# Where the last attention's shift and scale vectors are computed: VectorE in the second layer's MLP, or TensorE in the pooled layer's MLP

## The chip, the cores and the metric

The program runs on one core of a Trainium2 chip, in one launch. The metric is the device time of that core in microseconds (us), from the start of the program to its end; lower is better.

## The reference, cut to what matters

Two transformer blocks follow each other on 256 tokens of width 1024, all in float32. The first block has two layers (sparse attention, differential attention), the second has two as well: a pooling mixer, whose layer treats two streams of tokens (latent and context), and a grouped-query attention that reads both. Each layer has an MLP of its own. What is modulated is computed from a conditioning vector:

```python
mod = jax.nn.silu(c) @ ada_w[i] + ada_b[i]                                   # first block, one stream
sh1, sc1, g1, sh2, sc2, g2 = jnp.split(s_lat @ ada_w[i] + ada_b[i], 6, axis=-1)      # second block, latent
csh1, csc1, cg1, csh2, csc2, cg2 = jnp.split(s_ctx @ ada_w[i] + ada_b[i], 6, axis=-1)  # second block, context
a_l = modulate(rms_norm_2(h_lat, norm_g[i, 0]), sh1, sc1)
a_c = modulate(rms_norm_2(h_ctx, norm_g[i, 0]), csh1, csc1)
y_c, y_l = attn_mix(a_c, a_l, attn_w_qkv[j], attn_w_o[j], attn_q_g[j], attn_k_g[j], ctx_out)
```

So every layer needs six vectors of 1024 numbers, each the product of a vector of 1024 with a 1024x1024 matrix: 24 such products (numbered 0 to 23 below, six for each layer). For the last layer, vectors 18 and 19 (shift and scale ahead of the attention) are wanted for both streams, `c_2` and `c_ctx_2`; 20 to 23 for the latent stream alone.

## The kernel before, in words

The five engines run programs written by hand, with semaphores between them; nothing is reordered by a scheduler. The heavy work is a stream of weight **units** of 1 MB (128 partitions x 2048 floats). A unit goes through four stages: SyncE's queue loads it into one of four raw slots (`wraw`, `RAW_SLOTS`), ScalarE rounds it to `whi` (line 638, two halves), VectorE writes the rest `wlo = wraw - whi` (line 1161, two halves), and TensorE multiplies with three matmuls per product (high by high, high by low, low by high: lines 1980 to 1982). There are three slots for `whi` and `wlo`, so ScalarE may split unit u + 3 once TensorE has done unit u.

The MLPs are the segments `up0`, `down0` (first layer), `up1`, `down1` (second layer, 22 and 11 units), `up20`, `down20` (pooled layer, latent stream, 16 and 16), `up21`, `down21` (pooled layer, context stream) and `up3`, `down3` (last layer). Between `down1` and `up20` stand the two pooling products. `stream` is the loop of ScalarE and of VectorE over the units of a segment, `up_segment` and `down_segment` that of TensorE.

The 24 vector products are done in the gaps, in two ways. A product needs 4 MB of weights, in four pieces of 1 MB that take raw slots of the same ring as the units.
- By TensorE (`vector_units`, line 1927): a piece is 8 matmuls in plain fp32 with 32 columns, `cpad` (the conditioning vector, column 0 latent and column 1 context) against the raw weights; the four quarters of the output stand in four column groups of the array. TensorE waits for the piece to land, and the slot is free when the matmuls are done. Both streams come out of the same matmuls.
- By VectorE (`vector_rows`, lines 1104 and 1106, the vectors in `BY_VECTOR`): a piece is two instructions over 128x1024, which multiply a row block by the partition's number of `cpad` and add it to an accumulator in `work`. After four pieces `rows_sum` on TensorE (line 1908) adds up the partitions by 4 matmuls with the constant `first`.
Either way `vector_out` on VectorE (line 1086) then adds the bias to the result in PSUM bank 7 and writes `modrow`, and `columns` turns shift and scale to columns.

Where this happens is a table by hand: `HOSTED` (units of a segment after which a piece runs on TensorE), `ROWED` (VectorE's pieces), `SUMMED` (after which unit `rows_sum` comes) and `ADDED` (when `vector_out` comes). The function `hosting` sets by the same tables where in SyncE's queue (in order) the piece's transfer stands: for a piece at unit i, behind the transfer of unit i + 3. Before the change, vectors 18 and 19 are the eight pieces `HOSTED` in `up20`, at units 3, 4, 5, 6, 8, 9, 10 and 11. `up1` and `down1` hold no pieces.

## Time and profile before

| what | value |
|---|---|
| median of 3 runs | 1567.08 us (1566.0 to 1568.85) |
| the profiled execution | 1567.17 us, of which the span from first to last instruction is 1565.4 us |
| TensorE (matmul) busy | 1468.5 us (94%) |
| VectorE busy | 966.7 us (62%) |
| ScalarE busy | 759.3 us (49%) |
| mean granted TensorE clock | 0.979 |
| `up1`, from its zeroing matmul to that of `down1` | 568.2 to 699.0 us |
| `up20`, likewise | 807.0 to 923.0 us |
| `up21`, likewise | 1015.1 to 1112.2 us |

In the profile, busy matmul time overlaps: the duration of one is from its start to its modelled end, and several are in flight. What a unit costs is therefore read from the distance between events of neighbouring units. ScalarE's split of unit u + 3 is released by TensorE's last matmul of unit u, so the starts of line 638 in the timeline mark the ends of units on TensorE.

### The profile page before, as it was taken

To read this page: it belongs to the slowest core of one execution; us is meant where nothing else is said; L and a number is where in the kernel's file an instruction comes from. 1 tells how busy PE (TensorE), PEld (TensorE's weight loads), DVE (VectorE), ACT (ScalarE), POOL (GpSimd) and SP (SyncE) were. 2 spreads that over 40 slices of the span, in tenths; PEclk is the share of its full clock that TensorE was granted. 3 is DMA by queue.
4 is the path that set the end of the run, shared out by engine and by line. 5 is a ranking of instruction groups with operands and counts; after the bars stand their busy time and mean duration, and the time that the engine had idled before them with its cause. 6 is when DMAs were issued, how large, how long until landed. Compare 5 with 4: busy or idle time off the path is not lost.

```text
span 1565.4 us, 23725 instructions
## 1 busy us (share of the span) xinstructions
PE 1468.5 (94%) x9784; PEld 1250.5 (80%) x9784; DVE 966.7 (62%) x1537; ACT 759.3 (49%) x1197; POOL 22.1 (1%) x44
## 2 busy tenths in 40 slices
PE   4998899999999799999998999999999979899997
PEld 2775689998786589998877888799887756699886
DVE  3687565657787764456774447755577774554455
ACT  3525563334553554346464356455654535465543
POOL 1000000000000000000000000000000000000000
PEclk9999999999999799999999999999999989999999
DMA  9884787767757676554487955767466630255551
GB/s 348 277 280 162 245 268 248 264 237 288 287 183 274 259 253 224 176 179 156 137 295 273 320 189 213 267 210 247 166 229 228 215 108 1 81 162 188 170 200 48
DMA packets 174123, 334.76 MB, mean 214 GB/s; under 512 B 9656, under 2 KB 115648, under 8 KB 173888
## 3 DMA queue, kind: packets, MB, share of 16 engines
q1 hardware_dynamic: 172512, 331.52, 61.6%
q8 instruction: 78, 1.28, 0.3%
q0 software_dynamic: 1504, 1.72, 0.3%
q14 instruction: 29, 0.24, 0.0%
HBM read 332.17 MB, written 1.05 MB: 213 GB/s over the span
## 4 chain that ended last, share of the span: by engine, by line
PE 82%; DVE 10%; ACT 3%; DMA 3%; issue 2%; SPq 0%; DVEq 0%; ACTq 0%
PE ps L1980 24%; PE ps L1981 23%; PE ps L1982 23%; DVE wlo L1161 2%; PE ps L1927 2%; DMA wraw<-in_ada_w_dram 2%; PE ps L2178 1%; PE ps L2123 1%; DMA work<-in_ada_w_dram 1%; DVE res L1281 1%; DVE work L1279 1%; PE ps L2120 1%; ACT whi L638 1%; PE ps L2246 1%; PE ps L2210 1%
## 5 line engine op out<-in xcount | busy, mean ns | idle before, releaser
L1161 DVE TENSOR_TENSOR wlo<-wraw,whi 128x1024 fp32r<-128x1024 f32 (+1 forms) x424 | 497.4, 1216 | 321.3 <-ACT whi L638 320.8
L638 ACT ACTIVATE whi<-wraw 128x1024 fp32r<-128x1024 f32 (+1 forms) x424 | 421.7, 1045 | 383.2 <-PE ps L1982 347.7
L1980 PE MATMUL ps<-hT_hi,whi 128*128 128x256 f32 x1472 | 420.1, 285 | 0.5 <-DVE hT_lo L1353 0.5
L1981 PE MATMUL ps<-hT_lo,whi 128*128 128x256 f32 x1472 | 417.0, 283 | 0.0
L1982 PE MATMUL ps<-hT_hi,wlo 128*128 128x256 f32 x1472 | 416.9, 283 | 0.0
L1980 PEld LDWEIGHTS ps<-hT_hi,whi 128*128 128x128 f32 x1472 | 282.9, 192 | 9.1 <-issue 7.1
L1981 PEld LDWEIGHTS ps<-hT_lo,whi 128*128 128x128 f32 x1472 | 283.0, 192 | 0.0
L1982 PEld LDWEIGHTS ps<-hT_hi,wlo 128*128 128x128 f32 x1472 | 282.9, 192 | 0.0
L1980 PE MATMUL ps<-whi,act_hi 128*128 128x512 f32 x560 | 219.7, 392 | 0.0
L1982 PE MATMUL ps<-whi,act_lo 128*128 128x512 f32 x560 | 218.0, 389 | 0.0
L1981 PE MATMUL ps<-wlo,act_hi 128*128 128x512 f32 x560 | 217.9, 389 | 0.0
L1980 PE MATMUL ps<-whi,hT_hi 128*128 128x512 f32 (+2 forms) x416 | 162.7, 391 | 15.2 <-DVE hT_lo L1353 10.3
L1981 PE MATMUL ps<-wlo,hT_hi 128*128 128x512 f32 (+2 forms) x416 | 159.7, 384 | 0.0
L1982 PE MATMUL ps<-whi,hT_lo 128*128 128x512 f32 (+2 forms) x416 | 159.2, 383 | 0.0
L1980 PEld LDWEIGHTS ps<-whi,act_hi 128*128 128x128 f32 x560 | 105.1, 188 | 25.0 <-issue 3.7
L658 ACT ACTIVATE act_hi<-work 128x512 fp32r<-128x512 f32 x70 | 44.0, 629 | 164.9 <-PE ps L1982 164.9
L1168 DVE TENSOR_TENSOR act_lo<-work,act_hi 128x512 fp32r<-128x512 f32 x70 | 48.4, 692 | 121.7 <-ACT act_hi L658 121.4
L1982 PEld LDWEIGHTS ps<-whi,act_lo 128*128 128x128 f32 x560 | 105.1, 188 | 22.0
L1981 PEld LDWEIGHTS ps<-wlo,act_hi 128*128 128x128 f32 x560 | 105.1, 188 | 21.5
L1980 PEld LDWEIGHTS ps<-whi,hT_hi 128*128 128x128 f32 x416 | 79.9, 192 | 35.9 <-DVE hT_lo L1353 11.0
L1982 PEld LDWEIGHTS ps<-whi,hT_lo 128*128 128x128 f32 x416 | 79.8, 192 | 15.2
L1981 PEld LDWEIGHTS ps<-wlo,hT_hi 128*128 128x128 f32 x416 | 80.0, 192 | 14.3
(259 smaller groups left out, 1289.1 us busy)
## 6 DMA issues: line engine op xcount, KB each, us to landing
wraw<-in_mlp_w_dram SPq DMA_DIRECT2D x96, 1024.0 KB, 5.4
wraw<-in_ada_w_dram SPq DMA_DIRECT2D x78, 1024.0 KB, 5.7
wraw<-in_ffn_w_gate_dram SPq DMA_DIRECT2D x22, 1024.0 KB, 6.2
wraw<-in_ffn_w_up_dram SPq DMA_DIRECT2D x22, 1024.0 KB, 5.8
wraw<-in_ffn_w_down_dram SPq DMA_DIRECT2D x22, 1024.0 KB, 4.9
work<-in_ada_w_dram SPq DMA_DIRECT2D x18, 1024.0 KB, 9.9
wraw<-in_diff_w_in_dram SPq DMA_DIRECT2D x12, 1024.0 KB, 5.8
wraw<-in_attn_w_qkv_dram SPq DMA_DIRECT2D x12, 1024.0 KB, 5.2
```

The costliest lines, as they stand in the source:

```text
L638: nc.scalar.activation(whi[:, u % SPLIT_SLOTS, part], raw_view("w", u)[:, part], ACT.Copy).then_inc(hi_ready, 1)
L658: nc.scalar.activation(act_hi[:, d % 2, :], hid[:, 512 * i:512 * i + 512], ACT.Copy).then_inc(act_hi_ready, 1)
L1161: nc.vector.tensor_tensor(wlo[:, u % SPLIT_SLOTS, part], raw_view("w", u)[:, part], whi[:, u % SPLIT_SLOTS, part].bitcast(F32), ALU.subtra ...
L1168: nc.vector.tensor_tensor(act_lo[:, d % 2, :], hid[:, 512 * i:512 * i + 512], act_hi[:, d % 2, :].bitcast(F32), ALU.subtract).then_inc(act ...
L1279: nc.vector.tensor_tensor(tmp[:, t, cols], ps[:, D_BANKS[q], :], gate_b[:, cols], ALU.mult).then_inc(dve_emptied, 1)
L1281: nc.vector.tensor_tensor(res[:, strm, t, cols], res[:, strm, t, cols], tmp[:, t, cols], ALU.add).then_inc(sem("res_ready"), 1)
L1927: ins = mm(ps[32 * c_:32 * c_ + 32, ADA_BANK, 0:256], cpad[:, 0 if g < 12 else 1, kt, :], raw_view("a", r)[:, kk * D + 256 * c_:kk * D + 2 ...
L1980: mm(dst, s_hi, m_hi, start=start, stop=False, skip_group_check=skip)
L1981: mm(dst, s_hi, m_lo, start=False, stop=False, skip_group_check=skip)
L1982: return mm(dst, s_lo, m_hi, start=False, stop=stop, skip_group_check=skip)
L2120: ins = mm(ps[:, t_bank(n, b), (k % 2) * S:(k % 2 + 1) * S], xn[:, t, k * P:(k + 1) * P], mats[:, b, t, :], start=(t == 0), stop=(t == TT ...
L2123: ins = nc.tensor.transpose(ps[:, t_bank(n, b), (k % 2) * S + t * P:(k % 2) * S + (t + 1) * P], xn[:, t, k * P:(k + 1) * P], ident)
```

## The change

Vectors 18 and 19 join `BY_VECTOR`, with a row sum of their own for each stream (`BOTH`): a piece is now four VectorE instructions, two for each stream, and the sum is 8 matmuls in place of 4. `HOSTED` is gone. The pieces stand in `up1` (units 3, 6, 9, 12, 15, 18) and `down1` (units 5, 7), with the sums after unit 14 of `up1` and unit 9 of `down1`. As 18 and 19 now come ahead of 16 and 17, `IN_TURN` holds the new order of all vectors, for the waits on `mod_rows` and for the bias loads on GpSimd's queue. The constant `first` gets a 33rd column, so that a slice of it puts the sum in row 0 or row 1 of each group of 32. The two sums of a group of 32 columns follow each other directly (`for c_ ... for strm ...`). In `down20` and `down21` the sum moves from after unit 13 to after unit 14, its `vector_out` from 14 to 15.

```diff
-    put("first", np.tile((np.arange(32) == 0).astype(np.float32), (P, 1)))
+    put("first", np.tile((np.arange(33) == 1).astype(np.float32), (P, 1)))
...
-        BY_VECTOR = (7, 8, 9, 20, 21, 22, 23)
+        BY_VECTOR = (7, 8, 9, 18, 19, 20, 21, 22, 23)
+        BOTH = (18, 19)
+        IN_TURN = list(range(16)) + [18, 19, 16, 17, 20, 21, 22, 23]
...
-        HOSTED = {"up20": (3, 4, 5, 6, 8, 9, 10, 11)}
-        ROWED = {"up0": (3, 5, 7, 9, 11, 13, 15, 16), "down0": (0, 2, 4, 6), "up20": (3, 5, 7, 9), "down20": (6, 8, 10, 12),
+        ROWED = {"up0": (3, 5, 7, 9, 11, 13, 15, 16), "down0": (0, 2, 4, 6), "up1": (3, 6, 9, 12, 15, 18), "down1": (5, 7), "up20": (3, 5, 7, 9), "down20": (6, 8, 10, 12),
                  "up21": (2, 4, 6, 8), "down21": (6, 8, 10, 12)}
-        SUMMED = {"up0": (11, 18), "down0": (8,), "up20": (13,), "down20": (13,), "up21": (10,), "down21": (13,)}
-        ADDED = {"up0": (12, 19), "down0": (9,), "up20": (7, 12, 14), "down20": (14,), "up21": (11,), "down21": (14,)}
+        SUMMED = {"up0": (11, 18), "down0": (8,), "up1": (14,), "down1": (9,), "up20": (13,), "down20": (14,), "up21": (10,), "down21": (14,)}
+        ADDED = {"up0": (12, 19), "down0": (9,), "up1": (15,), "down1": (10,), "up20": (14,), "down20": (15,), "up21": (11,), "down21": (15,)}
...
+        def row_sums(g, strm):
+            return wk(5632 + 1024 * strm if g in BOTH else 11264 - 1024 * (BY_VECTOR.index(g) % 2), 1024)
...
-                if j == 0 and r >= 8:
+                if j == 0 and g == 19:
+                    dve.wait_ge(sem("rows_summed"), r // 4)
+                elif j == 0 and r >= 8:
                     dve.wait_ge(sem("rows_summed"), r // 4 - 1)
...
+                    for strm in range(2 if g in BOTH else 1):
+                        acc = row_sums(g, strm)
+                        by = cpad[:, 0 if g < 12 else 1, kt, strm:strm + 1]
+                        if kt == 0:
+                            ins = nc.vector.tensor_scalar(acc, w, by, None, ALU.mult)
+                        else:
+                            ins = nc.vector.scalar_tensor_tensor(out=acc, in0=w, scalar=by, in1=acc, op0=ALU.mult, op1=ALU.add)
...
+                strms = 2 if g in BOTH else 1
                 for c_ in range(4):
-                    ins = mm(ps[32 * c_:32 * c_ + 32, ADA_BANK, 0:256], const("first"), acc[:, 256 * c_:256 * (c_ + 1)], start=True, stop=True)
+                    for strm in range(strms):
+                        ins = mm(ps[32 * c_:32 * c_ + 32, ADA_BANK, 0:256], const("first")[:, 1 - strm:33 - strm], row_sums(g, strm)[:, 256 * c_:256 * (c_ + 1)],
+                                 start=(strm == 0), stop=(strm == strms - 1))
...
-                    if i in HOSTED.get(name, ()):
-                        vector_units()
```

On TensorE, between units 3 and 4 of `up20`, stood the first of the eight pieces. Before:

```order
L1982 MATMUL ps<-hT_hi,wlo 128x256
L1927 MATMUL ps<-wraw,cpad 32x256 [waits raw_full1,mod_ready,mod_rows]
L1927 MATMUL ps<-wraw,cpad 32x256 x7
L1980 MATMUL ps<-hT_hi,whi 128x256 [waits hact_done,lo_ready]
L1981 MATMUL ps<-hT_lo,whi 128x256
```

After, at the same place:

```order
L1990 MATMUL ps<-hT_lo,whi 128x256
L1991 MATMUL ps<-hT_hi,wlo 128x256
L1989 MATMUL ps<-hT_hi,whi 128x256 [waits hact_done,lo_ready]
L1990 MATMUL ps<-hT_lo,whi 128x256
L1991 MATMUL ps<-hT_hi,wlo 128x256
```

The eight matmuls and their wait for a landing are gone, here and at seven more places of `up20`.

On VectorE, in `up1` at unit 12, the split of the weights (`wlo`) is followed by the columns of an earlier vector (`modT`, `modA`). Before:

```order
L1161 TENSOR_TENSOR wlo<-wraw,whi 128x1024 [waits hi_ready] x2
L1143 COPY modT<-ps 128x2x4 [waits ada_turn]
L1143 COPY modT<-ps 128x2x4 x3
L1147 SCALAR_TENSOR_TENSOR modA<-modT,paramT 128x8 [waits dve_chain]
L1147 SCALAR_TENSOR_TENSOR modA<-modT,paramT 128x8
L1161 TENSOR_TENSOR wlo<-wraw,whi 128x1024 [waits hi_ready,mod_ready]
```

After:

```order
L1168 TENSOR_TENSOR wlo<-wraw,whi 128x1024 [waits hi_ready] x2
L1113 SCALAR_TENSOR_TENSOR work<-wraw,cpad,work 128x1024 [waits raw_full2]
L1113 SCALAR_TENSOR_TENSOR work<-wraw,cpad,work 128x1024
L1113 SCALAR_TENSOR_TENSOR work<-wraw,cpad,work 128x1024 [waits dve_chain]
L1113 SCALAR_TENSOR_TENSOR work<-wraw,cpad,work 128x1024
L1150 COPY modT<-ps 128x2x4 [waits ada_turn,rows_used]
L1150 COPY modT<-ps 128x2x4 x3
L1154 SCALAR_TENSOR_TENSOR modA<-modT,paramT 128x8 [waits dve_chain]
```

Four instructions and a wait for a landed piece stand ahead of the columns and of the next split.

On SyncE's queue, in `up1`, the transfers of the weights (`ffn_w_gate`, `ffn_w_up`) were alone. Before:

```order
L562 DMA wraw<-in_ffn_w_gate_dram 128x8x256 [waits lo_ready]
L562 DMA wraw<-in_ffn_w_up_dram 128x8x256 [waits lo_ready]
L562 DMA wraw<-in_ffn_w_gate_dram 128x8x256 [waits lo_ready]
L562 DMA wraw<-in_ffn_w_up_dram 128x8x256 [waits lo_ready]
L562 DMA wraw<-in_ffn_w_gate_dram 128x8x256 [waits lo_ready]
```

After:

```order
L579 DMA wraw<-in_ada_w_dram 128x2x1024 [waits lo_ready]
L566 DMA wraw<-in_ffn_w_up_dram 128x8x256 [waits lo_ready]
L566 DMA wraw<-in_ffn_w_gate_dram 128x8x256 [waits lo_ready]
L566 DMA wraw<-in_ffn_w_up_dram 128x8x256 [waits lo_ready]
L579 DMA wraw<-in_ada_w_dram 128x2x1024 [waits rows_used]
L566 DMA wraw<-in_ffn_w_gate_dram 128x8x256 [waits lo_ready]
```

Every fourth transfer is now a piece of the vectors, and from the second on it waits for VectorE to be done with the piece before it.

## Rows read from the trace of the kernel before

**Rows 1.** The page: busy time by engine, and the chain that ended last.
```profile
PE 1468.5 (94%) x9784; PEld 1250.5 (80%) x9784; DVE 966.7 (62%) x1537; ACT 759.3 (49%) x1197; POOL 22.1 (1%) x44
...
PE 82%; DVE 10%; ACT 3%; DMA 3%; issue 2%; SPq 0%; DVEq 0%; ACTq 0%
```
**Rows 2.** Windows: stretch, length, busy by engine, clock, DMA share, GB/s (`up1`, `up20`, `up21`).
```profile
568.20:699.00 130.80, 130.41 (x1074) 128.68 (x1073) 65.39 (x72) 59.10 (x71) 4.40 (x8) 1.00 0.65 214
...
807.00:923.00 116.00, 107.35 (x918) 98.46 (x918) 54.38 (x53) 56.72 (x77) 0.00 (x0) 0.99 0.79 272
...
1015.10:1112.20 97.10, 96.17 (x791) 93.92 (x791) 52.49 (x54) 51.09 (x67) 0.00 (x0) 1.00 0.66 217
```
**Rows 3.** Timeline of TensorE in `up20`: start, length, instruction, count of records, idle before.
```profile
833.21 1.07 PE L1927 MATMUL ps<-wraw,cpad 128*32 128x256 f32 x16
...
842.70 1.07 PE L1927 MATMUL ps<-wraw,cpad 128*32 128x256 f32 x16 [2.48 <-DMA wraw<-in_ada_w_dram]
...
858.91 1.07 PE L1927 MATMUL ps<-wraw,cpad 128*32 128x256 f32 x16 [2.25 <-DMA wraw<-in_ada_w_dram]
...
872.51 1.07 PE L1927 MATMUL ps<-wraw,cpad 128*32 128x256 f32 x16 [0.82 <-DVE modrow L1086]
...
888.64 1.93 PE L1927 MATMUL ps<-wraw,cpad 128*32 128x256 f32 x16 [2.17 <-DMA wraw<-in_ada_w_dram]
```
**Rows 4.** Windows again: the stretch around the last of these waits.
```profile
886.60:892.20 5.60, 3.56 (x24) 2.30 (x25) 2.36 (x2) 3.08 (x4) 0.00 (x0) 0.70 1.03 367
```
**Rows 5.** Timeline of ScalarE in `up20`: splits released by units 3, 4 and 12.
```profile
833.37 2.01 ACT L638 ACTIVATE whi<-wraw 128x1024 fp32r<-128x1024 f32 x2 [4.95 <-PE ps L1982]
840.31 2.00 ACT L638 ACTIVATE whi<-wraw 128x1024 fp32r<-128x1024 f32 x2 [2.81 <-PE ps L1982]
...
904.25 2.01 ACT L638 ACTIVATE whi<-wraw 128x1024 fp32r<-128x1024 f32 x2 [3.79 <-PE ps L1982]
```
**Rows 6.** Timeline of VectorE in `up1`, units 3 and 4.
```profile
596.19 2.36 DVE L1161 TENSOR_TENSOR wlo<-wraw,whi 128x1024 fp32r<-128x1024 f32 x2 [5.76 <-ACT whi L638]
598.47 0.69 DVE L1180 TENSOR_TENSOR work<-ps,hbuf 128x512 f32<-128x512 f32 x1
601.95 2.36 DVE L1161 TENSOR_TENSOR wlo<-wraw,whi 128x1024 fp32r<-128x1024 f32 x2 [2.80 <-ACT whi L638]
```
**Rows 7.** Timeline of ScalarE in `up0`, around a sum by 4 matmuls.
```profile
285.42 2.01 ACT L638 ACTIVATE whi<-wraw 128x1024 fp32r<-128x1024 f32 x2 [3.26 <-PE ps L1982]
291.94 2.01 ACT L638 ACTIVATE whi<-wraw 128x1024 fp32r<-128x1024 f32 x2 [4.51 <-PE ps L1982]
```
**Rows 8.** Timeline of TensorE: fp32 matmuls on two column groups, and on the whole array.
```profile
121.00 3.65 PE L2302 MATMUL ps<-wraw,work 128*32 128x256 f32 x32
...
777.42 7.07 PE L2120 MATMUL ps<-work 128*128 128x256 f32 x32
```
**Rows 9.** Instructions that read `cpad`: count, ns (least, median, most), first and last start.
```profile
L1106 DVE SCALAR_TENSOR_TENSOR work<-wraw,cpad,work x49: 1275/1284/1287, 244.1 to 1191.3; 128x1024 f32<-128x1024 f32 x49
```
**Rows 10.** The page, DMA issues: name, queue, count, KB each, us to landing.
```profile
wraw<-in_ada_w_dram SPq DMA_DIRECT2D x78, 1024.0 KB, 5.7
```
**Rows 11.** Timeline of VectorE, then of ScalarE, in `down1`, units 5 to 10.
```profile
743.03 0.69 DVE L1168 TENSOR_TENSOR act_lo<-work,act_hi 128x512 fp32r<-128x512 f32 x1 [3.20 <-ACT act_hi L658]
743.98 2.36 DVE L1161 TENSOR_TENSOR wlo<-wraw,whi 128x1024 fp32r<-128x1024 f32 x2 [0.26 <-ACT whi L638]
748.47 0.69 DVE L1168 TENSOR_TENSOR act_lo<-work,act_hi 128x512 fp32r<-128x512 f32 x1 [2.13 <-ACT act_hi L658]
...
769.12 0.68 DVE L1279 TENSOR_TENSOR work<-ps,gate_b 128x512 f32<-128x512 f32 x1
...
753.25 0.63 ACT L658 ACTIVATE act_hi<-work 128x512 fp32r<-128x512 f32 x1 [2.91 <-PE ps L1982]
```
**Rows 12.** Who waited for whom on TensorE, 990 to 1203 us: us, times, longest.
```profile
PE ps L1908 <- DVE work L1106: 2.4, 2, 1.2
```
**Rows 13.** Timeline of ScalarE at the end of `down21`: splits released by units 13 and 14.
```profile
1192.09 1.99 ACT L638 ACTIVATE whi<-wraw 128x1024 fp32r<-128x1024 f32 x2
1199.06 2.01 ACT L638 ACTIVATE whi<-wraw 128x1024 fp32r<-128x1024 f32 x2 [4.99 <-PE ps L1982]
```

More of the change, by code:

```diff
@@ L39 @@
 for _name, _n in (("ident", 128), ("causal", 256), ("cmp_neg", 32), ("cmp_ok", 32), ("ax_cos", 128), ("ax_sin", 128),
-                  ("inv_freq", 8), ("sel0", 128), ("sel1", 128), ("spread", 128), ("headmask", 512), ("first", 32)):
+                  ("inv_freq", 8), ("sel0", 128), ("sel1", 128), ("spread", 128), ("headmask", 512), ("first", 33)):
     CONST_COLS[_name] = (_at, _at + _n)
@@ L336, in hosting @@
             for i in range(by_name[name]["count"]):
-                if i in HOSTED.get(name, ()) or i in ROWED.get(name, ()):
+                if i in ROWED.get(name, ()):
                     units(by_name[name]["base"] + i + 4 - counted["w"])
-                if i in HOSTED.get(name, ()):
-                    extras(1)
                 if i in ROWED.get(name, ()):
@@ L366, in build @@
         extras(4)
+        hosting("up1")
+        hosting("down1")
         up_to("up20")
@@ L1044, in _ @@
                 bias(g)
-            for g in range(9, 21):
+            for g in IN_TURN[9:21]:
                 bias_after(g)
@@ L1077, in vector_out @@
                 for _ in range(n):
-                    g = vector_no[0]
+                    g = IN_TURN[vector_no[0]]
                     vector_no[0] += 1
@@ L1095, in vector_rows @@
                 raw_wait(dve, "v", r)
-                acc = wk(11264 - 1024 * (r // 4 % 2), 1024)
-                if j == 0 and r >= 8:
+                if j == 0 and g == 19:
+                    dve.wait_ge(sem("rows_summed"), r // 4)
+                elif j == 0 and r >= 8:
                     dve.wait_ge(sem("rows_summed"), r // 4 - 1)
@@ L1101, in vector_rows @@
                     w = raw_view("v", r)[:, kk * D:(kk + 1) * D]
-                    by = cpad[:, 0 if g < 12 else 1, kt, 0:1]
-                    if kt == 0:
-                        ins = nc.vector.tensor_scalar(acc, w, by, None, ALU.mult)
-                    else:
-                        ins = nc.vector.scalar_tensor_tensor(out=acc, in0=w, scalar=by, in1=acc, op0=ALU.mult, op1=ALU.add)
+                    for strm in range(2 if g in BOTH else 1):
[5 more added lines that the diff above has]
+                            ins = nc.vector.scalar_tensor_tensor(out=acc, in0=w, scalar=by, in1=acc, op0=ALU.mult, op1=ALU.add)
                     if kk == 0:
@@ L1903, in rows_sum @@
                 pe.wait_ge(sem("rows_used"), 4 * summed[0])
-                pe.wait_ge(mod_rows, g)
+                pe.wait_ge(mod_rows, IN_TURN.index(g))
                 bank7_wait()
-                acc = wk(11264 - 1024 * ((summed[0] - 1) % 2), 1024)
+                strms = 2 if g in BOTH else 1
                 for c_ in range(4):
-                    ins = mm(ps[32 * c_:32 * c_ + 32, ADA_BANK, 0:256], const("first"), acc[:, 256 * c_:256 * (c_ + 1)], start=True, stop=True)
+                    for strm in range(strms):
+                        ins = mm(ps[32 * c_:32 * c_ + 32, ADA_BANK, 0:256], const("first")[:, 1 - strm:33 - strm], row_sums(g, strm)[:, 256 * c_:256 * (c_ + 1)],
+                                 start=(strm == 0), stop=(strm == strms - 1))
                 ins.then_inc(sem("rows_summed"), 1)
@@ L1920, in vector_units @@
                         if g > 0:
-                            pe.wait_ge(mod_rows, g)
+                            pe.wait_ge(mod_rows, IN_TURN.index(g))
                         bank7_wait()
@@ L1965, in columns @@
                 assert EXTRA[extra_no[0] - 1][2] == 3 or EXTRA[extra_no[0] - 1] == ("cmp", 1, 1)
-                pe.wait_ge(mod_rows, last_vector[0] + 1)
+                pe.wait_ge(mod_rows, IN_TURN.index(last_vector[0]) + 1)
                 bank7_wait()
@@ L2056, in up_segment @@
                     hidden_unit(s_, i)
-                    if i in HOSTED.get(name, ()):
-                        vector_units()
                     if i in SUMMED.get(name, ()):
@@ L2170, in gate @@
                         emptied(n, t)
-                pe.wait_ge(mod_rows, 6 * l + 3 * f + 3)
+                pe.wait_ge(mod_rows, IN_TURN.index(6 * l + 3 * f + 2) + 1)
                 for h in range(2):
```

## The prediction, made before the changed kernel ran

> **What bounds the kernel now.** I first read the page: TensorE's matmuls are busy 94% of the span and make 82% of the chain that ended last, VectorE is busy 62% and ScalarE 49% [rows 1]. So a microsecond counts where it is TensorE's, work or wait; VectorE has room on the average, and the question is where. I then read windows over single MLPs [rows 2]. `up20` and `up21` are the same 16 units, but `up20` takes 116.0 us against 97.1, and TensorE is idle for 8.6 us of it. `up1` has nothing but its units: TensorE is busy for 130.4 of 130.8 us, VectorE for 65.4. The timeline of TensorE shows what is in the way in `up20` [rows 3]: the pieces of vectors 18 and 19, and ahead of four of them an idle time, 2.48, 2.25, 0.82 and 2.17 us. Three of the four end with the landing of the piece's own transfer. After the last, the granted clock is 0.70 over a stretch of 5.6 us [rows 4], and the same 16 records take 1.93 us in place of 1.07.
>
> **Part 1: the eight pieces leave `up20`.** The splits of ScalarE mark the ends of TensorE's units. From the end of unit 3 to that of unit 12 it is 904.25 - 833.37 = 70.88 us [rows 5], with nine units and all eight pieces between. A unit alone takes 5.76 us: in `up1`, VectorE's splits of neighbouring units start at 596.19 and 601.95 [rows 6]. Nine are 51.8 us, so the pieces cost 19.0. This divides into eight times 1.18 for the matmuls (the first piece: 840.31 - 833.37 - 5.76) or 9.4, the four idle times, 7.7, and 1.9 left over, mostly the low clock. All of it is between units on TensorE, with no cover: **-19.0 us**. Check: 116.0 - 19.0 = 97.0, and `up21`, which already has four one-stream pieces on VectorE, a sum and four transposes more, takes 97.1. The four pieces of vector 20 stay in `up20` and were there before.
>
> **Part 2: two sums come to TensorE's path.** A sum by 4 matmuls costs 0.76 us between units (291.94 - 285.42 - 5.76) [rows 7]. Eight matmuls in two rounds of four column groups cost 1.18, so a further round costs 0.42. That the round is one matmul long shows elsewhere: 16 matmuls (32 records, two each) on two column groups take 3.65 us, 0.46 for each pair, and 16 on the whole array 7.07, 0.44 each [rows 8]. The new sum has 8 matmuls, but in the order group 0, group 0, group 1, group 1 and so on. No row shows this order. Below: if group 1 may start while the second of group 0 waits, two rounds, 1.18. Above: one after the other, 0.34 + 8 x 0.44 = 3.9. I take the case in which a waiting matmul holds up those behind it: the second of a group then runs beside the first of the next, five rounds, 0.34 + 5 x 0.43 = 2.5. It is also about the middle. The sums stand between units, in `up1` after unit 14 and in `down1` after unit 9: **+5.0 us** (2.4 to 7.8). The Trainium skill ("TensorE: Matmul & The Clock Gate", Part 3, Packing small matmuls) states that matmuls are strictly first in, first out, in start and in end, and only weight loads are pulled ahead. By it a sum is 2.5 us and the total as here; if matmuls passed each other it would be 1.2 and the total 2.6 less. No row of this trace has the order that would tell.
>
> **Part 3: VectorE's pieces in `up1`, taken at nothing.** A piece is four instructions of 1.284 us [rows 9], 5.2 with the wait in its middle (the first of each vector is cheaper). Three units, the distance of two pieces, give VectorE 3 x 2.36 for splits, 1.5 x 0.69 for products and 5.2: 13.3 of 17.3 us. In detail at unit 3: it ends at 595.1 (half a split of ScalarE, 1.1, ahead of 596.19), VectorE is through with split and product at 599.15, the piece lasts to 604.3, and the split of unit 7, which stood at 601.95, ends at 606.7. TensorE wants it at 595.1 + 3 x 5.76 = 612.4. The cover is thus 5.7 us, and if it were gone, each microsecond over would be one of TensorE's. Behind the piece on VectorE stand that split and, at unit 12, the columns of vectors 12 and 13, which the sum after unit 14 waits for with 2 us to spare. On SyncE's queue a piece waits for its slot, from the second on for the piece before to be used, and the weights stand behind it. Unit 10's transfer takes the slot of unit 7, free at 606.7; with 5.7 us to land [rows 10] it is there at 612.4, wanted by ScalarE at the end of unit 7, 618.1. Again 5.7 us. GpSimd's bias loads in the new order wait for columns that are made before `up1` starts; ScalarE's program is the same. All at 0.
>
> **Part 4: VectorE's pieces in `down1`, taken at nothing.** Here a unit is 5.44 us (748.47 - 743.03) [rows 11] and the cover thinner. The split at 743.98 ends at 746.3, the piece at 751.5, and the rest of the activations of unit 8 (`act_lo`, at 748.47 before) at 752.3. TensorE wants it when unit 7 ends, at 753.2 (the start of ScalarE at 753.25): 0.9 us to spare. The second piece runs from 757.6 to 762.8, ahead of the end of unit 9 at 764.1, where the sum wants it, by 1.3. VectorE then comes to the residual some 1.0 us later than 769.12 (0.6 from late splits, 0.4 for `vector_out`). TensorE itself comes 2.5 later there because of the sum, counted above, so this adds nothing; if the sum were 1.2 it would just cover it.
>
> **Part 5: the sum moved in `down20` and `down21`.** TensorE waits there for VectorE's last piece, 1.2 us each time [rows 12]. One unit later the piece is long done. In `down20` the wait goes, 1.2. In `down21` units 13 and 14 stand 1199.06 - 1192.09 = 6.97 us apart [rows 13], 1.53 over 5.44; what follows is VectorE's split and residual, released by the end of unit 14, which now has no sum ahead of it: 1.5. `vector_out` stands in the same place of VectorE's program as before, since no split lies between: **-2.7 us** (0 to -3.1).
>
> **The sum.** -19.0 + 5.0 - 2.7 = -16.7 against the profiled execution's 1567.17 us, of which 1565.4 is span: 1550.5. The median is 0.1 below that execution, so **1550.4 us**.
>
> **The rivals.**
> A. The matmuls of the sums pass each other. For it: in rows 3 four groups run together, 16 records in 1.07. Against it: there each group's next matmul comes only after the other groups' first. Sums of 1.2: 1550.4 - 2.6 = 1547.8.
> B. VectorE holds up TensorE in `up1` or `down1`. For it: 0.9 us in `down1`, where the transfers, the splits and the pieces meet; against it: the 1284 ns vary by 12 at most over 49 instructions. Overruns of 2 to 6 us: 1552.4 to 1556.4.
> C. The change doesn't do what it says: the idle times of `up20` come from the ring of four slots, which vector 20's pieces still share, and not from the pieces on TensorE. Then 7.7 + 1.9 stay: 1560.0. Against it: `up21` has the same four pieces on the same ring, and its unit times add up to 97.1.
> D. Slower. In `up1` the weight transfers stand in SyncE's queue behind pieces that wait for VectorE. From the point at which a piece takes over 10.9 us on VectorE (5.2 and the cover of 5.7), TensorE pays the rest at each of eight places. Equal to before is reached 16.7 / 8 = 2.1 us later, at 13.0 us a piece, 2.5 times what rows 9 say; at 13.5 it would be 1571. Nothing in the rows speaks for it but the untried order of the queue.
>
> **The chances.** Forecast (1549.0 to 1552.4) 0.63; A 0.15; B 0.13; C 0.05; D 0.02; something unseen 0.02, half of it slower. The range that holds 8 in 10 takes in A and most of B: 1547.0 to 1555.0. A measurement of this kernel can tell about 0.2%, 3.1 us, from no change; faster by more than that 0.96, within it 0.01, slower 0.03.
>
> **What the changed profile would show.** Part 1: `up20` lasts 97 us, with no matmul on `cpad` in it and no idle time of TensorE over 0.5 us inside; the granted clock stays at 1.00. Part 2: the splits of ScalarE around unit 14 of `up1` and unit 9 of `down1` stand 2.5 us further apart than 5.76 and 5.44 (1.2 for rival A, 3.9 at the most). Part 3: `up1` lasts 133.3 us with TensorE waiting for no `wlo`. Part 4: `down1` is longer by 2.5 only, and no wait for `act_lo`. Part 5: no wait of the sum for VectorE in `down20` and `down21`. The prediction is wrong if `up1` or `down1` show waits of TensorE on VectorE or on a transfer, or if `up20` stays over 100 us.

## The result, and the profile after

| | kernel before | changed kernel |
|---|---|---|
| median, same chip | 1567.96 us (1566.0 to 1572.12, 4 runs) | 1547.36 us (1546.8 to 1547.86, 4 runs) |
| profiled execution, and its span | 1567.17, 1565.4 us | 1546.80, 1545.0 us |

The ratio is 0.9862, 95% interval [0.9848, 0.9876]: faster by 20.6 us. The forecast was 16.7, and by the ratio the time is 0.9862 x 1567.08 = 1545.5 us, below the low end of the range (1547.0). On another chip, beside later runs, the same kernel gave 0.9874 [0.9859, 0.9889]. The sign and the place of the gain were as forecast; its size was short by 3 to 5 us, by which of these one takes.

The page after, busy time by engine and the chain that ended last, answers to [rows 1]:

```profile
PE 1457.7 (94%) x9688; PEld 1246.3 (81%) x9688; DVE 1003.7 (65%) x1569; ACT 759.3 (49%) x1197; POOL 22.1 (1%) x44
...
PE 85%; DVE 8%; ACT 3%; DMA 2%; issue 1%; SPq 0%; DVEq 0%; ACTq 0%
```

TensorE has 96 records fewer, VectorE 37 us more work (32 instructions), and TensorE's share of the chain rose from 82 to 85%.

Windows over `up1`, `up20` and `up21` of the changed kernel, each from one zeroing matmul to the next segment's: length, busy by engine, clock, DMA share, GB/s. They answer to [rows 2]:

```profile
568.03:700.07 132.04, 131.65 (x1091) 129.22 (x1090) 92.92 (x97) 59.10 (x71) 4.40 (x8) 1.00 0.77 260
809.44:906.67 97.23, 96.30 (x791) 93.91 (x791) 53.70 (x51) 56.74 (x77) 0.00 (x0) 1.00 0.71 236
997.58:1094.63 97.05, 96.12 (x790) 93.91 (x790) 51.69 (x53) 51.07 (x67) 0.00 (x0) 1.00 0.64 214
```

`up20` has gone from 116.07 us, by the same cut, to 97.23 and looks like `up21`; its clock is 1.00. `up1` grew from 130.82 to 132.04, by 1.2 only, although VectorE's work in it grew from 65.4 to 92.9 us. The same cuts around the other changed places are `down1` with the pooling behind it, `down20`, and from the start of `down21` to that of `up3`. The first fence is the kernel before, the second the changed kernel.

```profile
699.04:806.89 107.85, 103.65 (x589) 82.03 (x589) 73.42 (x136) 53.12 (x93) 1.10 (x2) 0.97 0.54 186
922.96:1015.14 92.18, 90.97 (x413) 73.92 (x413) 65.77 (x80) 49.13 (x70) 0.00 (x0) 1.00 0.66 229
1112.17:1371.20 259.03, 233.44 (x1109) 187.54 (x1109) 172.64 (x289) 129.98 (x201) 0.00 (x0) 0.96 0.42 146
```
```profile
700.07:809.44 109.37, 104.09 (x605) 82.31 (x604) 83.42 (x145) 53.20 (x93) 1.10 (x2) 0.97 0.58 204
906.67:997.58 90.91, 90.91 (x412) 73.96 (x413) 66.53 (x81) 49.15 (x70) 0.00 (x0) 1.00 0.69 234
1094.63:1351.14 256.51, 232.63 (x1108) 187.31 (x1109) 172.94 (x289) 129.95 (x201) 0.00 (x0) 0.96 0.42 148
```

So the span's 20.4 us are made up of `up1` +1.2, `down1` and pooling +1.5, `up20` -18.8, `down20` -1.3, `down21` to `up3` -2.5, and -0.5 in the stretches without a change.

The new sum on TensorE is shown twice. First comes the line of its matmuls in a stretch of 25 us of `up1` and one of 60 us of `down1` (length, busy and records, clock, DMA share, GB/s), then the timeline of ScalarE's splits around the end of unit 14 of `up1`, which answers to [rows 7]:

```profile
655.00:680.00 25.00, 1.09 (x16) 1.00 0.72 240
740.00:800.00 60.00, 1.09 (x16) 1.00 0.59 210
```
```profile
658.71 2.01 ACT L642 ACTIVATE whi<-wraw 128x1024 fp32r<-128x1024 f32 x2 [3.74 <-PE ps L1991]
665.68 2.01 ACT L642 ACTIVATE whi<-wraw 128x1024 fp32r<-128x1024 f32 x2 [4.48 <-PE ps L1991]
671.44 2.01 ACT L642 ACTIVATE whi<-wraw 128x1024 fp32r<-128x1024 f32 x2 [3.75 <-PE ps L1991]
```

Eight matmuls (16 records) keep TensorE busy for 1.09 us, and the two splits between which they stand in `up1` are 6.97 us apart, 1.21 over a unit's 5.76. That is two rounds of four, not the five that the prediction took. VectorE at units 3 and 4 of `up1`, against [rows 6]:

```profile
596.02 2.36 DVE L1168 TENSOR_TENSOR wlo<-wraw,whi 128x1024 fp32r<-128x1024 f32 x2 [5.77 <-ACT whi L642]
598.30 0.69 DVE L1187 TENSOR_TENSOR work<-ps,hbuf 128x512 f32<-128x512 f32 x1
598.90 1.41 DVE L1111 TENSOR_SCALAR work<-wraw,cpad 128x1024 f32<-128x1024 f32 x2
600.35 2.48 DVE L1113 SCALAR_TENSOR_TENSOR work<-wraw,cpad,work 128x1024 f32<-128x1024 f32 x2
602.86 2.36 DVE L1168 TENSOR_TENSOR wlo<-wraw,whi 128x1024 fp32r<-128x1024 f32 x2
```

The first piece of a vector takes 3.9 us, later ones 5.0; the split behind it ends at 605.2, 7.0 us before TensorE wants it (612.2, three units behind the split of ScalarE at 594.93). Over `up1` and `down1` (568 to 769 us) the list of who waited for whom on TensorE has a single row, and it was there before:

```profile
PE ps L1989 <- DVE hT_lo L1360: 0.2, 1, 0.2
```

The next lines are of `down1`: VectorE's activations of unit 8 behind the first piece, and its second piece, then ScalarE, against [rows 11]:

```profile
752.31 0.69 DVE L1175 TENSOR_TENSOR act_lo<-work,act_hi 128x512 fp32r<-128x512 f32 x1
...
758.17 4.99 DVE L1113 SCALAR_TENSOR_TENSOR work<-wraw,cpad,work 128x1024 f32<-128x1024 f32 x4
...
754.27 0.63 ACT L662 ACTIVATE act_hi<-work 128x512 fp32r<-128x512 f32 x1 [2.91 <-PE ps L1991]
...
759.71 0.63 ACT L662 ACTIVATE act_hi<-work 128x512 fp32r<-128x512 f32 x1 [2.91 <-PE ps L1991]
760.25 1.99 ACT L642 ACTIVATE whi<-wraw 128x1024 fp32r<-128x1024 f32 x2
765.15 2.01 ACT L642 ACTIVATE whi<-wraw 128x1024 fp32r<-128x1024 f32 x2 [2.91 <-PE ps L1991]
```

`act_lo` is there at 753.0, TensorE is through with unit 7 at 754.3. The second piece ends at 763.16, 2.0 us before the end of unit 9 at 765.15. The last two lines are ScalarE's at the end of `down21`, against [rows 13]:

```profile
1174.59 1.99 ACT L642 ACTIVATE whi<-wraw 128x1024 fp32r<-128x1024 f32 x2
1179.49 2.01 ACT L642 ACTIVATE whi<-wraw 128x1024 fp32r<-128x1024 f32 x2 [2.91 <-PE ps L1991]
```

They stand 4.90 us apart, where it was 6.97. Between 906 and 1203 us TensorE waits for no sum, where [rows 12] had 2.4 us.

### The profile page after: what moved, and what is told of

It is laid out like the page before. It is cut to its first block, busy times and chain, and to the rows that moved or that the text cites. A ratio compares the mean times of both kernels' runs of the same rounds, so it can differ in the third digit from the quotient of the medians.

```text
span 1545.0 us, 23575 instructions
## 1 busy us (share of the span) xinstructions
PE 1457.7 (94%) x9688; PEld 1246.3 (81%) x9688; DVE 1003.7 (65%) x1569; ACT 759.3 (49%) x1197; POOL 22.1 (1%) x44
## 4 chain that ended last, share of the span: by engine, by line
PE 85%; DVE 8%; ACT 3%; DMA 2%; issue 1%; SPq 0%; DVEq 0%; ACTq 0%
PE ps L1989 25%; PE ps L1990 24%; PE ps L1991 24%; PE ps L1936 1%; PE ps L2185 1%; DVE wlo L1168 1%; PE ps L2130 1%; DMA work<-in_ada_w_dram 1%; DVE res L1288 1%; PE ps L2127 1%; DVE work L1286 1%; PE ps L2253 1%; PE ps L2217 1%; ACT work L880 1%; PE ps L2197 1%
## 5 line engine op out<-in xcount | busy, mean ns | idle before, releaser
L1113 DVE SCALAR_TENSOR_TENSOR work<-wraw,cpad,work 128x1024 f32<-128x1024 f32 x77 | 97.5, 1281 | 1.3
```

The lines of the kernel that those rows point to most:

```text
L1113: ins = nc.vector.scalar_tensor_tensor(out=acc, in0=w, scalar=by, in1=acc, op0=ALU.mult, op1=ALU.add)
```

## The experiments

The theory says that the gain is the removal of TensorE's pieces and their idle time, that the sums are cheap because matmuls of different column groups pass each other (theory P, rival A of the prediction), and that VectorE's pieces are covered. The rivals are that the order is held and the sum is cheap for another reason, or that the difference to the forecast comes from the moved sums of Part 5, from the wider `first`, or from the place rather than the engine. Where an experiment has one execution, it is read from its trace, and its time stands beside it only.

### 1. The order of the sums' matmuls

In `up1` the sum goes round by round over the four groups; in `down1` it keeps the changed kernel's order, but is issued four times over.

```diff
-                for c_ in range(4):
-                    for strm in range(strms):
+                if g == 18:
+                    order = [(c_, s_) for s_ in range(2) for c_ in range(4)]
+                elif g == 19:
+                    order = [(c_, s_) for c_ in range(4) for s_ in range(2)] * 4
...
+                for c_, strm in order:
```

> The changed kernel with other orders of the matmuls in its two two-stream sums. In up1 all four column groups of stream 0, then the four of stream 1 (the changed kernel has both streams of a group in a row, and there the gap between the splits of units 14 and 15 was 1.20 us longer than a unit). In down1 the changed kernel's own order, but the eight matmuls issued four times over (32). Theory P (matmuls on different column groups pass a waiting one): up1 again 1.2 us; down1 8 rounds of 0.43 and 0.34, 3.8 us. Theory F (strictly in order, the 1.20 being luck of another kind): up1 1.2, down1 17 rounds, 7.7 us.

Measured: 1550.44 us (one execution, beside 1568.58 of the kernel before). The line of the sum's matmuls in the same two stretches of `up1` and `down1`:

```profile
655.00:680.00 25.00, 1.07 (x16) 1.00 0.74 239
740.00:800.00 60.00, 3.73 (x64) 1.00 0.54 188
```

In `up1` the order makes no difference: 1.07 against 1.09 us. In `down1` 32 matmuls take 3.73 us, eight rounds of 0.47, although each group's two stand in a row. Of the 2.6 us more, 1.0 reaches `up20`: counted from the split at the end of `down1`, the first split of the pooling comes 2.63 later than in the changed kernel (at 796.61 us), and the next one, at 815.02, has 1.66 of it back. So the sum in `down1` is only partly on the path.

### 2. How many may wait

Both sums are now issued four times over, in `up1` with eight in a row on each group, in `down1` round by round. The edit is shown against that of experiment 1.

```diff
                 if g == 18:
-                    order = [(c_, s_) for s_ in range(2) for c_ in range(4)]
+                    order = [(c_, s_) for c_ in range(4) for _ in range(4) for s_ in range(2)]
                 elif g == 19:
-                    order = [(c_, s_) for c_ in range(4) for s_ in range(2)] * 4
+                    order = [(c_, s_) for s_ in range(2) for c_ in range(4)] * 4
```

> The changed kernel with each two-stream sum issued four times over (32 matmuls). In up1 eight matmuls in a row on one column group, then eight on the next; in down1 round by round over the four groups. Theory P with no limit to how many may stand waiting: both 3.8 us. Theory P with room for two in each group: up1 about 26 rounds, 11.5 us, down1 3.8. Theory F: up1 29 rounds, 12.8 us, down1 3.8. So up1 tells how far a matmul may pass others.

Measured: 1562.25 us (one execution). The same view as above comes first, then the timeline of TensorE's line of the sum in `up1`, from 661 us on (the count is of records; this view begins behind the first two of the 64), then that of ScalarE's splits before and behind it:

```profile
655.00:680.00 25.00, 11.50 (x64) 1.00 0.46 149
740.00:800.00 60.00, 3.66 (x64) 1.00 0.48 165
```
```profile
660.70 11.04 PE L1921 MATMUL ps<-work,cst 128*32 128x256 f32 x62
...
660.41 2.00 ACT L642 ACTIVATE whi<-wraw 128x1024 fp32r<-128x1024 f32 x2 [3.74 <-PE ps L1996]
677.79 2.01 ACT L642 ACTIVATE whi<-wraw 128x1024 fp32r<-128x1024 f32 x2 [14.90 <-PE ps L1996]
```

The same 32 matmuls take 3.66 us round by round and 11.50 with eight in a row. The splits agree, though the ends of matmuls are modelled: they stand 17.38 us apart, 11.62 over a unit. By 0.34 + 0.43 a round, 11.5 us are 26 rounds. All one after the other would be 32 rounds, all in parallel 8. If each group takes two (one that runs, one that waits) and a third stops the queue, a group's last two run beside the next group's first two: 8 + 3 x 6 = 26. The expectation had this number for a depth of two, but that the depth is two is inferred from these orders alone. What is shown is that a matmul that waits for its own group does not hold up those of other groups, and that this ends somewhere between two and eight in a row.

### 3. The moved sums alone, in the kernel before

```diff
-        SUMMED = {..., "down20": (13,), "up21": (10,), "down21": (13,)}
-        ADDED = {..., "down20": (14,), "up21": (11,), "down21": (14,)}
+        SUMMED = {..., "down20": (14,), "up21": (10,), "down21": (14,)}
+        ADDED = {..., "down20": (15,), "up21": (11,), "down21": (15,)}
```

> The kernel before with one part of the change alone: in down20 and down21 the sum after unit 14 in place of 13, its vector_out at 15 in place of 14. The prediction's step had 2.7 us less. From the trace of the changed kernel I now expect 1.3 in down20 and 2.0 in down21, 3.3 us less in all. Rival: the 1.2 us waits of TensorE alone go, 2.4 us less.

Measured: 1567.49 us (10 runs) against 1568.58, ratio 0.9986 [0.9976, 0.9996], which is a gain of 0.6 to 3.8 us. The trace is sharper. It shows the splits at the end of `down21`:

```profile
1195.01 1.99 ACT L638 ACTIVATE whi<-wraw 128x1024 fp32r<-128x1024 f32 x2
1199.91 2.01 ACT L638 ACTIVATE whi<-wraw 128x1024 fp32r<-128x1024 f32 x2 [2.91 <-PE ps L1982]
```

They stand 4.90 apart again in place of the 6.97 of [rows 13], a step of -2.07. In `down20` the same step is -2.07, and +0.80 comes back one unit later, where the sum now stands. Together that is -3.35 (3.3 was expected from the trace of the changed kernel), and the changed kernel has the same three steps.

### 4. The wider constant alone, in the kernel before

```diff
-                  ("inv_freq", 8), ..., ("headmask", 512), ("first", 32)):
+                  ("inv_freq", 8), ..., ("headmask", 512), ("first", 33)):
...
-                    ins = mm(ps[32 * c_:32 * c_ + 32, ADA_BANK, 0:256], const("first"), ...
+                    ins = mm(ps[32 * c_:32 * c_ + 32, ADA_BANK, 0:256], const("first")[:, 0:32], ...
```

> The kernel before with the constant first one column wider, of which the same 32 columns of value are used: all small tiles lie 32 bytes further on, as in the changed kernel, and nothing else differs. The changed kernel's trace is shorter by some 1.0 us ahead of up1, in the last attention and at the start of up3, where neither its instructions nor their order changed. Theory L (it is the place of the tiles in memory): 1.0 us less, 1566.2. Theory N (it is the spread from one execution to the next): no difference beyond 0.3 us.

Measured: 1569.61 us (12 runs) against 1568.58, ratio 1.0004 [0.9991, 1.0016]. The wider constant has no effect that can be told.

### 5. The place without the engine

Vectors 18 and 19 stay on TensorE, 8 matmuls a piece, but in `up1`.

```diff
-        BY_VECTOR = (7, 8, 9, 18, 19, 20, 21, 22, 23)
+        BY_VECTOR = (7, 8, 9, 20, 21, 22, 23)
...
+        HOSTED = {"up1": (3, 5, 7, 9, 14, 15, 16, 17)}
-        ROWED = {..., "up1": (3, 6, 9, 12, 15, 18), "down1": (5, 7), ...
+        ROWED = {...
...
```

> The changed kernel with vectors 18 and 19 given back to TensorE, as before the change, but in up1 (pieces after units 3, 5, 7, 9, 14, 15, 16 and 17) in place of up20; the sums for them and VectorE's pieces are gone. It parts the two halves of the change, another place and another engine. Theory S (a piece on TensorE costs 1.18 us, and the other 9.6 us of the 19.0 in up20 came from the ring of slots that vector 20's four pieces fill as well): up1 has no other pieces, so the pieces cost 9.4 us there; against the changed kernel + 9.4 - 2.5 = 6.9 us more, 1554.3. Theory E (a piece on TensorE always waits for its landing as in up20, since its slot is held until TensorE itself is through): 19.0 in up1 too, 1563.9.

Measured: 1553.32 us (1551.77 to 1554.86), beside 1569.33 of the kernel before, ratio 0.9892 [0.9877, 0.9907]. The time is that of theory S. Windows over `up1`, `down1` with the pooling, and `up20`:

```profile
569.25:709.53 140.28, 139.90 (x1203) 132.40 (x1202) 66.07 (x74) 58.98 (x71) 4.39 (x8) 1.00 0.79 260
709.53:816.30 106.77, 102.05 (x590) 80.86 (x589) 72.71 (x134) 52.77 (x92) 1.10 (x2) 0.98 0.53 184
816.30:913.74 97.44, 96.28 (x791) 93.93 (x790) 54.41 (x53) 57.15 (x78) 0.00 (x0) 1.00 0.73 243
```

`up1` is 9.46 us longer than before, 8 x 1.18, and TensorE waits there for no piece, although four of them stand at neighbouring units as in `up20`. So the matmuls cost what [rows 5] say, and the waits and the low clock belong to `up20`. Vector 20's pieces share the ring there, but whether that is the reason was not tested apart.

By the trace the move of the place alone is worth -18.6 in `up20` and +9.5 in `up1`, together -9.2. The moved sums (experiment 3, kept here) make it -12.5, and the spans of the two profiled executions differ by 12.8. The medians differ by 16.0, as the kernel before took 1569.33 beside these runs and not 1567.17; these 3 us have no cause found.

That VectorE does the pieces is worth -8.2 more in `up1` (140.28 to 132.04), -0.2 in `up20` and +2.6 in `down1` (106.77 to 109.37), -5.8 by the trace and 3 to 5 us by the ratios (0.9892 to 0.9874 or 0.9862). `down1` with the pooling is 1.1 shorter here than in the kernel before. The difference lies in the last 11 to 12 us ahead of `up20`, where the granted clock was 0.84 in place of 0.71.

### 6. How thick VectorE's cover is

All eight pieces are in `up1`, in two groups at four units in a row, and both sums stand there.

```diff
-        ROWED = {..., "up1": (3, 6, 9, 12, 15, 18), "down1": (5, 7), ...
+        ROWED = {..., "up1": (3, 4, 5, 6, 15, 16, 17, 18), ...
-        SUMMED = {..., "up1": (14,), "down1": (9,), ...
-        ADDED = {..., "up1": (15,), "down1": (10,), ...
+        SUMMED = {..., "up1": (14, 21), ...
+        ADDED = {..., "up1": (15,), "down1": (0,), ...
```

> The changed kernel with VectorE's eight pieces all in up1, at units 3, 4, 5, 6 and 15, 16, 17, 18 (sums after 14 and 21). It tests the cover of up1. A unit with a piece is 2.36 + 5.2 + 0.35 = 7.9 us on VectorE against 5.76 on TensorE, so it falls behind by 2.15 each. Theory M (the prediction's margins: 5.7 us before TensorE waits for a split, and the weights' transfers wait behind the pieces): after four pieces 8.6 us behind, less 5.7, so TensorE waits some 2 to 3 us in each group, 4 to 6 in all. Theory R (ring: with a piece at each unit only half of the four slots hold weights, and SyncE's queue is in order): each piece costs TensorE a part of a landing of 5.7 us, over 10 us in all. If VectorE's cover is deeper than I think: 0.

Measured: 1548.22 us (one execution), span 1546.4. Windows over `up1`, and `down1` with the pooling:

```profile
569.58:702.62 133.04, 132.66 (x1106) 129.67 (x1105) 101.08 (x105) 59.96 (x72) 4.39 (x8) 1.00 0.80 267
702.62:810.40 107.78, 102.85 (x593) 81.86 (x589) 74.96 (x139) 52.33 (x93) 1.10 (x2) 0.97 0.57 195
```

`up1` is 2.2 us longer than before, less than two sums (2.4), so pieces in a row cost TensorE nothing net. Expected were waits of 4 to 6 us. The split behind the first piece ends 7.0 us before TensorE wants it and the one behind the fourth, at 629.27, 1.8 us before (631.03). The expectation took all four pieces off a cover of 5.7 that the prediction had worked out behind one piece, so it counted the first twice. Transfers do come late to ScalarE here: three of its splits wait for a weight to land, the worst starts 1.3 us late, and TensorE waits for none of them. The sum moved out of `down1` takes 1.6 us off that stretch (109.37 to 107.78) and adds 1.0 to `up1` (132.04 to 133.04).

### 7. VectorE's pieces twice as long

Ahead of each of the four instructions of a piece of 18 and 19 stands another `scalar_tensor_tensor`, whose output nothing uses. By the trace a piece then takes 10.0 us in place of 5.0 (the first of a vector 9.0 in place of 3.9).

```diff
+                        if g in BOTH:
+                            again = nc.vector.scalar_tensor_tensor(out=wk(11264, 1024), in0=w, scalar=by, in1=w, op0=ALU.mult, op1=ALU.add)
...
```

> The changed kernel with four more instructions of 128x1024 in each piece of vectors 18 and 19, whose results go unused: a piece takes VectorE 10.4 us in place of 5.2. Theory M (margins as predicted, 5.7 us over a piece of 5.2 in up1 and 0.9 in down1): up1 as before to within 0.5 us; in down1 TensorE waits 4.3 us at unit 8 for act_lo, and some more at the second piece and the sum behind it, 4 to 8 us in all; 1551 to 1555. Rival (up1's VectorE has no room for 10.4 us each three units: 18.5 of 17.3): up1 longer by 3 us or more.

Measured: 1561.12 us (one execution), span 1559.3. Windows over `up1`, and `down1` with the pooling, and who waited for whom on TensorE, 568 to 830 us (us, times, longest):

```profile
568.70:705.69 136.99, 133.22 (x1090) 130.80 (x1090) 119.56 (x120) 59.10 (x71) 4.39 (x8) 0.99 0.72 241
705.69:823.57 117.88, 107.53 (x605) 84.39 (x605) 95.18 (x155) 53.16 (x93) 1.09 (x2) 0.95 0.57 200
```
```profile
PE ps L1993 <- DVE act_lo L1179: 3.9, 1, 3.9
...
PE ps L1920 <- DVE modA L1158: 3.4, 1, 3.4
PE ps L1920 <- DVE work L1117: 1.1, 1, 1.1
```

Both stretches are longer than expected, `up1` by 4.95 us where 0.5 at most was expected, `down1` with the pooling by 8.5 where it was 4 to 8. In `up1` the splits hold with pieces of twice the length: TensorE waits for none, and the one behind the piece at unit 9 ends at 646.7, 0.7 us before it is wanted (647.4). What is late is what the sum after unit 14 waits for, the columns of an earlier vector (`modA`), as they read the same PSUM bank. These are the columns in the changed kernel and here, and the window of TensorE behind the wait here (length, busy by engine, clock, DMA share, GB/s):

```profile
655.59 0.24 DVE L1154 SCALAR_TENSOR_TENSOR modA<-modT,paramT 128x8 f32<-128x8 f32 x2
...
662.28 0.24 DVE L1158 SCALAR_TENSOR_TENSOR modA<-modT,paramT 128x8 f32<-128x8 f32 x2
...
664.00:668.00 4.00, 4.00 (x23) 4.00 (x23) 3.79 (x4) 0.00 (x0) 0.00 (x0) 0.59 0.96 342
```

Unit 14 ends at 658.71 in the changed kernel, 2.9 us behind the columns, and at 659.39 here, 3.1 us ahead of them. The wait is 3.4 us, and the clock of 0.59 behind it makes most of the other 1.5 of `up1`. The prediction gave that place 2 us of room and the splits 5.7. In `down1` it is `act_lo`, as it said; the sum there waits 1.1 for its piece as well, and the clock falls to 0.95.

### 8. One vector more on VectorE

Vector 16, which TensorE does in 32 matmuls between the pooling products, goes to `up1` as well; pieces then stand at every second unit, and the sums after 11 and 19.

```diff
-        BY_VECTOR = (7, 8, 9, 18, 19, 20, 21, 22, 23)
-        BOTH = (18, 19)
+        BY_VECTOR = (7, 8, 9, 18, 19, 16, 20, 21, 22, 23)
+        BOTH = (16, 18, 19)
-        ROWED = {..., "up1": (3, 6, 9, 12, 15, 18), "down1": (5, 7), ...
+        ROWED = {..., "up1": (3, 5, 7, 9, 11, 13, 15, 17, 19, 21), "down1": (5, 7), ...
...
-        SUMMED = {..., "up1": (14,), "down1": (9,), ...
+        SUMMED = {..., "up1": (11, 19), "down1": (9,), ...
...
-            vector_units(4)
...
```

> A step further: vector 16 too (both streams) by VectorE's row sums, its four TensorE pieces between the two pooling products gone. Pieces at every second unit of up1 from 3 to 21 (ten) and at units 5 and 7 of down1, sums after 11 and 19 of up1 and 9 of down1. In the changed kernel vector 16's pieces take 3.6 us between the pooling products, and TensorE then waits for the landings of vector 17's. Theory T: one more sum, 1.2 us, against 3.6 and a part of the waits, up to 7 us: 2.4 to 6 us less than the changed kernel, 1541.5 to 1545. VectorE has 2 x 2.36 + 0.69 + 5.2 = 10.6 of 11.5 us for two units. Rival V: this is too tight, TensorE waits in up1, and the result is 1547 or above. Rival N: the norm behind the second product is bound by VectorE's residual and vector 17's pieces hide behind it either way, so the 3.6 us alone come back: 1545.

Measured: 1550.31 us (1548.09 to 1551.54), ratio 0.9869 [0.9851, 0.9887]. Windows over `up1`, and `down1` with the pooling, and the first row of TensorE's waits:

```profile
569.20:708.13 138.93, 134.54 (x1107) 131.22 (x1106) 106.81 (x110) 59.09 (x71) 4.40 (x8) 0.99 0.81 270
708.13:813.24 105.11, 100.33 (x542) 80.88 (x541) 87.78 (x148) 53.07 (x93) 1.10 (x2) 0.97 0.54 183
```
```profile
PE ps L1976 <- DVE modrow L1088: 4.0, 1, 4.0
```

The time is not the expected 1541.5 to 1545, and by the ratio it can't be told from that of the changed kernel. The vector leaves the pooling (109.37 to 105.11, -4.3), but `up1` is 6.9 longer than in the changed kernel. One sum more is 1.2 of it; the rest is one wait of 4.0 us and the low clock behind it (0.50 from 654 to 656 us). `columns` at unit 12 stands on TensorE right behind the sum after unit 11, and needs `vector_out`, which VectorE reaches only after a piece and a split.

### 9 and 10. The changed kernel again, and that wait taken out

```diff
-        COLUMNS_AT = {("up0", 14): (1, 0), ("up1", 12): (2, 0), ("up21", 5): (3, 0)}
+        COLUMNS_AT = {("up0", 14): (1, 0), ("up1", 10): (2, 0), ("up21", 5): (3, 0)}
```

> The changed kernel itself once more, beside the next kernel and on its chip. The trace comparison gives 20.4 us less than before, of which 19.0 + 3.35 - 2.4 = 19.95 have a cause found in the runs (the eight pieces, the sums moved in down20 and down21, the two new sums); the rest of 0.5 is taken for the spread of the first 230 us and of the last attention, which differ by up to 2 us between traces of kernels that are the same there. If so, the ratio to before is 0.9872, within 0.0012.

> vector_16_too with one edit: the columns of vectors 12 and 13 come after unit 10 of up1 in place of 12, ahead of the first two-stream sum (after unit 11). In vector_16_too TensorE waited 4.0 us at these columns for the vector_out of vector 18, which stands on VectorE behind a piece, and up1's step there was 4.5 us more than a sum. Theory W (this wait alone was what made it slower): 4.5 us less than vector_16_too, about 1.8 less than the changed kernel, ratio to before 0.986. Rival V (VectorE is too full with a piece at every second unit): the wait moves to the sums after 11 and 19, and the gain over the changed kernel stays away or is a loss.

Measured beside the same runs of the kernel before (1568.37 us): the changed kernel 1548.27 (1547.8 to 1548.7), ratio 0.9874 [0.9859, 0.9889]; with vector 16 and the columns two units earlier 1546.57 (1545.85 to 1547.19), 0.9862 [0.9845, 0.9878]. Windows of the latter over `up1`, `down1` with the pooling, and `up20`:

```profile
568.73:702.26 133.53, 132.92 (x1106) 129.82 (x1106) 106.67 (x110) 59.06 (x71) 4.39 (x8) 1.00 0.84 281
702.26:807.36 105.10, 99.46 (x541) 80.66 (x541) 87.74 (x148) 53.07 (x93) 1.10 (x2) 0.98 0.54 182
807.36:905.89 98.53, 97.60 (x790) 95.18 (x790) 53.70 (x51) 56.84 (x77) 0.00 (x0) 0.98 0.71 234
```

The wait of 4.0 us is gone (`up1` 138.93 to 133.53, 5.4 less with the clock). Against the changed kernel the two cuts ahead of `up20` are 2.8 us shorter and `up20` is 1.3 longer, at a clock of 0.98: 1.5 us in sum, 1.7 by the medians. That is what theory W expected (1.8). The four runs of the one all lie below the four of the other beside them, but the gain is 0.1%, the two intervals overlap, and the changed kernel's first runs had the same ratio, 0.9862. That it is the faster kernel is not shown; that the wait was what made experiment 8 slow is.

## Why the prediction was right or wrong

**Part 1, the eight pieces: right.** Forecast -19.0 and `up20` at 97 us; measured -18.8 and 97.23, with a clock of 1.00. Of TensorE's waits within it one is left, 0.8 us for `hbuf` at its end, which the forecast's "none over 0.5" did not have, though the kernel before has it too. Experiment 5 shows the split: 9.4 for the matmuls, wherever they stand, the rest for the waits and the low clock in this place. Rival C, by which the idle times stay when the pieces go, is excluded by the 97.23.

**Part 2, the two sums: the step that failed.** The term of +5.0 us was mis-sized. It took "a waiting matmul holds up those behind it", five rounds, 2.5 us each; measured are two rounds, 1.2 us between the splits in `up1` and 1.1 us of busy time in `down1`, where no split shows the cost. Rival A, with 0.15 given to it, was the right one, and its 2.6 us are most of what was missing. The bound below (1.18) was worked out from the rows and hit; the choice above it was not borne out by any row. The rule of the Trainium skill ("TensorE: Matmul & The Clock Gate", Part 3, Packing small matmuls) that matmuls start and end strictly first in, first out does not hold here across column groups: by an estimate in its sense the order of experiment 1 would make 17 rounds of the 32 matmuls in `down1` (each pair starts beside the second of the pair before), 0.34 + 17 x 0.43 = 7.7 us, and 3.73 were measured. The same estimate gives 29 rounds, 12.8 us, for `up1` of experiment 2, where 11.50 were measured. The measurement decides.

**Part 3, VectorE in `up1`: right in the sum.** No wait of TensorE, and `up1` is 1.2 longer, which is its sum. The cover of the splits was the 5.7 us stated: experiment 7 uses up 5.0 more a piece and leaves 0.7. The columns ahead of the sum had their 2 us in the prediction, but it named no case in which they give way. They were the thinnest place of `up1` (2.9 us measured), gave way first and cost 4.9 us with the clock behind them. Of rival D (the queue of SyncE) this much shows: in experiments 6 and 7 single splits of ScalarE wait for a landing and start up to 1.3 us late, and TensorE waits for none of them. Its own point, 10.9 us a piece, lies above the 10.0 of experiment 7, so beyond that it wasn't tried.

**Part 4, VectorE in `down1`: right.** No wait for `act_lo`; it was 1.3 us early where 0.9 was forecast, since four instructions in a row take 4.99 us and not 5.2. The second piece ended 2.0 us ahead of the sum (1.3 forecast). With doubled pieces `act_lo` is late by 3.9 us and this stretch 8.5 us longer: rival B named the right place, but its condition, a piece that overruns, was not met in the changed kernel.

**Part 5, the moved sums: right in kind, 0.6 too small.** Forecast -2.7, measured -3.35 (experiment 3). The base was wrong. The prediction subtracted 5.44, a unit of `down1` between splits that both stand behind an `act_hi` (759.71 and then 760.25 above) and so start 0.54 late. The last split of a segment has none ahead and comes 4.90 us after its neighbour. So each wait and sum made 2.07, not 1.53, and in `down20` 0.80 of it came back with the sum, where the prediction had left 0.33.

**The sum by what was measured.** Parts 1 to 5 are -18.8 (`up20`), +2.7 (`up1`, and `down1` with the pooling) and -3.35, or -19.5; the span moved by -20.4. The remaining 0.9 stands in places with the same instructions, 0.5 of it outside the cuts above and 0.4 within those of `down20` and from `down21` on. The two traces of the changed kernel differ there as well: `up0` begins at 212.36 us in one and at 214.24 in the other, and the spans are 1545.0 and 1546.9. It stays open which part of 0.9 is more than this spread.

**The range.** Rival A with Part 5's own bound (-3.1) is 1547.4, so every case that was weighed lies above the low end, 1547.0, and the first median, 1547.36, does too. But the kernel before took 1567.96 beside it, not 1567.08, and by the ratios the times are 1545.5 and 1547.3. The end stood too close for a reason that no term of the sum could show: two executions of equal code differ by 2 us, and the range had no room for it. Even with both sums at 1.2 and Part 5 at 3.35, the forecast's own sum is -19.95, or 1547.1 us, barely inside.

## What to carry to other kernels

The small matmuls of this kernel (fp32, 32 columns, 256 elements) on different column groups of the array cost by rounds as long as no more than two in a row went to one group; eight in a row cost three times as much as round by round. Orders between two and eight were not tried. When a side job is moved off the busiest engine, ask first what its place costs: of the 19 us that the pieces took in `up20`, 9 were saved by the move to a stretch without waits alone, with the job still on TensorE. List a margin for each thing that stands behind the moved work, since the thinnest decides: in `up1` with longer pieces it was the columns that free the shared PSUM bank, not the weight splits. And a forecast needs room for the spread between executions of the same code.

## What the runs showed of the hardware

- TensorE: 32 fp32 matmuls with 32 columns and 256 moving elements took 3.66 us round by round over four groups, 3.73 with two in a row per group, 11.50 with eight in a row.
- VectorE: `scalar_tensor_tensor` in fp32 on 128x1024 took 1.28 us alone; four in a row on two accumulators took 4.98 to 4.99 us.
- TensorE's clock: behind a wait of 3.4 us of TensorE the granted clock was 0.59 from 664 to 668 us and 1.00 from 668 to 672 (experiment 7), behind one of 4.0 us it was 0.50, the level of 1.2 GHz, from 654 to 656 us (experiment 8).
- A constant one column wider changed nothing: 1.0004 [0.9991, 1.0016].
- Equal instructions up to `up0` ended 1.9 us apart in two executions of the changed kernel (212.36 and 214.24 us).
